# A hybrid decoder layer on one core: attention, sample and recurrent work woven between the input projections

## What is computed

```python
h = rmsnorm(x, g_mix)
z = h @ w_in                      # 1024 -> 8704 columns: xr, gr, q, k, v, g_lru, g_att
xc = causal_conv(xr)              # width 4
yr = rglru(xc, h0, w_rg_a, w_rg_x)          # gates, then a scan over time
b_lru = (yr * gelu(gr)) @ w_br_lru
q, k = rope(rmsnorm(q)), rope(rmsnorm(k))   # 12 heads of 128 each
att, kv_new = attend(q, k, v)     # 3 groups of 4 heads; samples read a cache of 1024 positions
b_att = att @ w_br_att
x = x + (sigmoid(g_lru) * b_lru + sigmoid(g_att) * b_att) @ w_out
x = x + moe(rmsnorm(x))           # top-4 of 32 experts, 12.6 MB of weights each
x = x + sigmoid(rmsnorm(x) @ w_ple_gate) * (p @ w_ple)
```

## Time and profile before

| | us |
|---|---|
| median of 3 runs (1495.41 to 1503.62) | 1499.1 |
| the profiled execution's own time | 1501.54 |
| its span, first to last instruction | 1499.7 |
| TensorE busy in it | 1367.6 (91%) |
| VectorE, ScalarE busy | 390.7, 200.4 |
| bytes moved by DMA | 530.44 MB |

### The profile page before, as it was taken

How to read it: one execution, slowest core, us unless ns; L and a number is a source line. 1 busy time by engine, 2 the same in 40 slices (tenths; PEclk the granted TensorE clock), 3 DMA queues, 4 the chain that set the end, 5 groups by cost and what they waited for, 6 DMA issues and landing times.

```text
span 1499.7 us, 16237 instructions
## 1 busy us (share of the span) xinstructions
PE 1367.6 (91%) x6662; PEld 703.2 (47%) x6662; DVE 390.7 (26%) x529; ACT 200.4 (13%) x344; POOL 18.5 (1%) x31
## 2 busy tenths in 40 slices
PE   6999996977998899999999999999999999999848
PEld 5887885866776333333333333333333333333227
DVE  2014944074223212122112212112112122121123
ACT  1113110252301110110110110110101101100001
POOL 0000000020000000000000000000000000000000
PEclk9999998998999999999999999999999999999969
DMA  9688899466445999999999999999999999999910
GB/s 374 275 333 271 297 335 365 174 214 199 193 186 210 385 412 427 428 429 428 427 429 428 428 428 428 429 428 428 428 429 429 427 428 428 429 428 428 426 49 29
DMA packets 40077, 530.44 MB, mean 354 GB/s; under 512 B 5997, under 2 KB 6141, under 8 KB 10693
## 3 DMA queue, kind: packets, MB, share of 16 engines
q1 hardware_dynamic: 36992, 470.67, 75.6%
q10 hardware_dynamic: 1685, 54.43, 9.4%
q0 software_dynamic: 1360, 4.76, 1.4%
HBM read 525.08 MB, written 58.38 MB: 389 GB/s over the span
## 4 chain that ended last, share of the span: by engine, by line
DMA 47%; PE 46%; DVE 3%; issue 2%; ACT 1%; another core or an unknown queue 0%; ACTq 0%; SPq 0%; DVEq 0%
DMA ring<-in_wexp 43%; PE PS L734 16%; PE PS L495 13%; DMA ring<-in_win 4%; PE PS L656 3%; PE PS L873 2%; PE PS L674 2%; PE PS L780 1%; PE PS L506 1%; PE PS L538 1%; PE PS L749 1%; PE PS L602 1%; DVE ring L1171 1%; PE PS L706 1%; PE PS L522 0%
## 5 line engine op out<-in xcount | busy, mean ns | idle before, releaser
L734 PE MATMUL PS<-ring,Zb 128*64 128x512 f32 x3072 | 687.3, 597 | 42.5 <-DMA ring<-in_wexp 39.3
L734 PEld LDWEIGHTS PS<-ring,Zb 128*64 128x64 f32 x3072 | 210.7, 137 | 469.9 <-issue 371.2
L495 PE MATMUL PS<-hT,ring 128*128 128x264 f32 x1024 | 233.8, 392 | 11.6 <-DMA ring<-in_win 11.6
L495 PEld LDWEIGHTS PS<-hT,ring 128*128 128x128 f32 x1024 | 197.9, 194 | 47.1 <-issue 12.5
L1374 DVE COPY Zb<-PS 64x512 f32<-64x512 f32 x32 | 21.9, 683 | 317.7 <-PE PS L734 317.7
L1037 ACT ACTIVATE Zb<-Zb 128x512 f32<-128x512 f32 x32 | 20.1, 629 | 449.5 <-DVE Zb L1352 449.5
L780 PE MATMUL PS<-Zb 128*128 128x264 f32 x256 | 75.7, 419 | 3.9 <-DVE xc L1342 2.4
L1342 DVE TENSOR_TENSOR xc<-xc,PS 128x528 f32<-128x528 f32 x68 | 47.7, 701 | 109.0 <-PE PS L780 102.1
L780 PEld LDWEIGHTS PS<-Zb 128*128 128x128 f32 x256 | 44.1, 192 | 59.4 <-issue 48.7
L1029 ACT ACTIVATE Zb<-PS 128x512 f32<-128x512 f32 x32 | 19.1, 597 | 362.8 <-PE PS L763 362.8
L1363 DVE TENSOR_SCALAR Zb<-PS 128x512 f32<-128x512 f32 x32 | 22.1, 691 | 155.2 <-PE PS L734 155.2
(11 more groups left out here) (228 smaller groups left out, 825.7 us busy)
## 6 DMA issues: line engine op xcount, KB each, us to landing
ring<-in_wexp SPq DMA_DIRECT2D x192, 2048.0 KB, 24.4
ring<-in_win SPq DMA_DIRECT2D x17, 2048.0 KB, 15.6
out_kvs<-in_cache ACTq DMA_DIRECT2D x8, 4032.0 KB, 25.1
out_kvs<-in_cache ACTq DMA_DIRECT2D x8, 1984.0 KB, 12.7
ring<-in_kt SPq DMA_DIRECT2D x2, 2048.0 KB, 14.7
ring<-in_cache SPq DMA_DIRECT2D x2, 2048.0 KB, 8.6
ring<-in_w_br_lru SPq DMA_DIRECT2D x2, 2048.0 KB, 14.9
ring<-in_w_out SPq DMA_DIRECT2D x2, 2048.0 KB, 14.9
```

Source lines behind the costliest of these rows:

```text
L495: last = mm(PS[:, t, 0:T], w[:, k, t * P:(t + 1) * P], hT[:, k, :], start=(k == 0), stop=(k == KT - 1))
L734: last = mm(PS[CAP * h:CAP * (h + 1), bank, :], src[:, k, f:f + CAP], w[:, k, h * CH:(h + 1) * CH], start=(not seeded and slot % 2 == 0 an ...
```

## The change

The parts of the program that stood one after the other are threaded through the projection. What it does, in the order of the program:

- The columns of z come as q, k, x, v, gate, merge gates. Three ring slots carry `w_in`; the fourth (`stream`, slot 3) carries one after another the cached keys of the three groups, the gate weights, the cached values of the three groups, and half of w_br_lru.
- q and k are normalized and rotated apart (`normed(0)`, `normed(1)`), each with its own sums on TensorE after tiles 13 and 25. The convolution comes behind both on VectorE.
- The samples are spread over four column groups, 8 rows of each in use; their scores stand after tiles 25, 28 and 31, their values in attention rounds 1 to 3.
- The key rows stand after tile 39, gates and value rows after tile 43. ScalarE, no longer VectorE, copies the rows out.
- Each attention round holds three of the last 24 projection tiles: scores, two tiles, transposes, one tile, product with v. The recurrent stage is spread over VectorE's and ScalarE's rounds.
- b_lru now comes before b_att, and the merged sum is made tile by tile, so that w_out starts on the first.
- Two cache copies of 4 MB and the three remainder copies move from ScalarE's queue ahead of the experts to SyncE's queue behind the first tile of the last projection; four of the other 4 MB copies move to later points.
- `further` nests its four tests, so that the first that fails skips all.
- At the end the last experts' sums use four PSUM banks in place of two (`SPREAD_AT`), ScalarE scales x tile by tile for the last projection, VectorE adds the eight squares so that one matmul sums them, and seven banks (`PG_AT`) take the projection.

The diff, cut to its core:

```diff
-ZQ, ZK, ZX, ZGR, ZV, ZGL, ZGA, NZ = 0, 12, 24, 32, 40, 52, 60, 68
+ZQ, ZK, ZX, ZV, ZGR, ZGL, ZGA, NZ = 0, 12, 24, 32, 44, 52, 60, 68
+RING = (5, 3, 2, 0, 1, 4)
+SPREAD_AT = (2, 0, 2, 0)
+PG_AT = (5, 6, 7, 0, 1, 2, 3, 5)
...
-            for c in range(1, NCHUNK):
+            def passes(c):
                 with eng.If(eng.value_load(most, min_val=0, max_val=T) > c * CAP):
...
+                    if c + 1 < NCHUNK:
+                        passes(c + 1)
+            passes(1)
...
# SyncE
+            def piece(p):
+                if p >= 3:
+                    sp.wait_ge(S.z_done, 4 * (p - 2))
+                win(p, p % 3).then_inc(wins[p % 3], 16)
+            sp.dma_start(kts[0], a["kt0"]).then_inc(S.kt0_in, 16)
+            for p in range(3, 9):
+                piece(p)
+            sp.wait_ge(S.ss_mm, 1)
+            sp.dma_start(kts[1], a["kt1"]).then_inc(S.kt1_in, 16)
+            piece(9)
+            sp.wait_ge(S.ss_mm, 2)
+            sp.dma_start(kts[2], a["kt2"]).then_inc(S.kt2_in, 16)
+            piece(10)
+            sp.wait_ge(S.ss_mm, 3)
+            sp.dma_start(stream, a["wrg"]).then_inc(S.wrg_in, 16)
+            for p in range(11, 14):
+                piece(p)
+            sp.wait_ge(S.gate_mm, 16)
+            sp.dma_start(vts, cached_v(0)).then_inc(S.v0_in, 16)
+            piece(14)
+            sp.wait_ge(S.spv_mm, 1)
+            sp.dma_start(vts, cached_v(1)).then_inc(S.v1_in, 16)
+            piece(15)
+            sp.wait_ge(S.spv_mm, 2)
...
+            sp.wait_ge(S.pg_mm, 1)
+            for g in range(NG):
+                shift_rest(sp, g)
+            for b in range(EARLY, NS):
+                shift(sp, 2, b)
...
# TensorE
+            z_tiles(4, 14)
+            qk_sums(0)
+            z_tiles(14, 26)
+            qk_sums(1)
+            stream_scores(0)
+            z_tiles(26, 29)
+            stream_scores(1)
+            z_tiles(29, 32)
+            stream_scores(2)
+            z_tiles(32, 36)
+            pe.wait_ge(S.ss_prod, 1)
...
+            z_tiles(36, 40)
+            token_rows(0)
+            z_tiles(40, 44)
+            gates()
+            token_rows(1)
+            for it in range(8):
+                n = STEP + 3 * it
+                scores(it)
+                z_tile(n)
+                z_tile(n + 1)
+                turn(it)
+                z_tile(n + 2)
+                weigh(it)
+                if 1 <= it <= 3:
+                    stream_values(it - 1)
...
-            pe.wait_ge(S.merged, 1)
+                            pe.wait_ge(S.merged, k + 1)
...
# ScalarE, ahead of the experts and at the end
-            for b in range(EARLY, NS):
-                shift(2, b)
-            for g in range(NG):
-                shift_rest(g)
...
+            for k in range(KT):
+                act.wait_ge(S.added, 2 * E + 1 + k // 2)
+                A(hT[:, k, :], xc[:, k, :], ACT.Copy, scale=feat[:, k, FGP:FGP + 1]).then_inc(S.hp_ok, 1)
```

More of the change, by code:

```diff
@@ L400, in _ @@
-            half(a["w_br_lru"], 0, wbl[0], S.wbl_in)
-            half(a["w_br_lru"], 4, wbl[1], S.wbl_in)
-            half(a["w_out"], 0, wout[0], S.wout_in)
-            sp.wait_ge(S.ba_mm, KT)
+            piece(0)
+            sp.dma_start(cst[:, :], a["cst"]).then_inc(S.cst_in, 16)
+            piece(1)
+            piece(2)
+            sp.dma_start(gqk[:, :], a["gqk"]).then_inc(S.rope_in, 16)
+            sp.wait_ge(S.xgain, 1)
+            sp.wait_ge(S.sq_ok, 1)
+            sp.dma_start(rope, a["rope"]).then_inc(S.rope_in, 16)
@@ new lines, in _ @@
+            piece(16)
+            sp.wait_ge(S.spv_mm, 3)
+            half(a["w_br_lru"], 0, wbl[0], S.wbl_in)
+            sp.wait_ge(S.z_done, 4 * 15)
+            half(a["w_br_lru"], 4, wbl[1], S.wbl_in)
+            sp.wait_ge(S.z_done, 4 * 16)
+            half(a["w_br_att"], 0, wba, S.wba_in)
+            sp.wait_ge(S.z_done, NZ)
+            half(a["w_out"], 0, wout[0], S.wout_in)
+            sp.wait_ge(S.at_pv, 8)
+            sp.wait_ge(S.tk_out, 16 * KV_STORES)
+            sp.wait_ge(S.vt_out, 16 * KV_STORES)
@@ L555, in _, with qk_sums @@
-            for g in range(NG):
-                last = mm(PS[0:32, 5, g:g + 1], prod[:, g * 32:(g + 1) * 32], ones[:, 0:1], start=True, stop=True)
-            last.then_inc(S.ss_rows, 1)
-            n = 0
-            for z0 in (ZK, ZV):
+            def qk_sums(m):
+                pe.wait_ge(S.sq_qk, m + 1)
+                for c in range(7):
+                    i = 7 * m + c
+                    n = min(CH, 12 * T - c * CH)
+                    if i >= 3:
+                        pe.wait_ge(S.qkn_ev, i - 2)
+                    mm(PS[:, 4 + i % 3, 0:n], ones, sq_qk[m][:, c * CH:c * CH + n], start=True, stop=True).then_inc(S.qkn_mm, 1)
@@ L570, in _, with gates @@
                         n += 1
+            def gates():
+                pe.wait_ge(S.wrg_in, 16)
+                pe.wait_ge(S.conv_done, 1)
+                pe.wait_ge(S.tk_ev, 9)
+                for j in range(KT):
+                    for m in range(2):
+                        n = 2 * j + m
+                        if n >= 3:
+                            pe.wait_ge(S.gate_ev, n - 2)
+                        for c in range(2):
+                            last = mm(PS[:, 4 + n % 3, 0:T], wrg[:, m, j // 2, c, (j % 2) * P:(j % 2 + 1) * P],
+                                      xc[:, 2 * (j // 2) + c, :], start=(c == 0), stop=(c == 1))
+                        last.then_inc(S.gate_mm, 1)
             def scores(it):
@@ L584, in scores, with turn @@
                 last.then_inc(S.at_sc, 1)
[L586 to L588 removed]
+            def turn(it):
                 pe.wait_ge(S.at_p, it + 1)
@@ L641, in _ @@
-            pe.wait_ge(S.spv_ev, 1)
-            pe.wait_ge(S.at_s, 8)
-            for g in range(NG):
-                last = mm(PS[:, 0, 0:32], pvrows[:, :], ident[0:96, 32 * g:32 * g + 32],
-                          start=(g == 0), stop=(g == NG - 1))
-            last.then_inc(S.spv_sum, 1)
-            def dense(weights, arrived, src, nk, done, evac, base=1):
+                if 1 <= it <= 3:
+                    stream_values(it - 1)
+                if it == 5:
+                    pe.wait_ge(S.spv_ev, 1)
+                    nc.tensor.transpose(PS[:, 7, 0:P], pvrows[:, :], ident).then_inc(S.spv_sum, 1)
@@ L650, in dense @@
+            def dense(weights, src, nk, done, evac, bank):
                 for m in range(KT):
@@ new lines, in _ @@
+            evacs(14, 16)
+            both(3)
+            evacs(16, 20)
+            both(4)
+            evacs(20, 24)
+            both(5)
+            evacs(24, 26)
+            qk_roots(1)
+            evacs(26, 28)
+            both(6)
+            evacs(28, 32)
+            both(7)
+            evacs(32, 36)
+            shift(act, 2, 0)
+            evacs(36, 40)
+            rows_out(0)
+            shift(act, 2, 1)
+            evacs(40, 44)
+            act.wait_ge(S.sp_exp, 1)
+            act.wait_ge(S.ss_rows, 1)
```

706 lines of the change are left out of this document (352 added, 354 removed).

## The result

The changed kernel takes 1480.3 us (median of 4 runs, 1477.3 to 1481.3) against 1498.5 for the kernel before, run on the same chip. The ratio is 0.987, with a 95% interval of 0.985 to 0.990: faster by 1.3%. The forecast was 1452, so the sign and the range were right and less than half of the gain came: 18 us in place of 47.

A forecast was written before the change was run, and what follows sets the result against it. The experts were taken as a DMA-bound block of fixed length, with TensorE's chain ahead of it setting its start. Gains of 25.6 (front), 2 (experts) and 19.5 (tail) summed to 47.1 us, giving 1452 us, range 1430 to 1483.

The forecast's parts named there:

- the term on the second group's values: Attention rounds: cached values land in 19.3 us behind one 4 MB copy; TensorE waits 6.6, plus 2.6 of slow clock.
- a first expert product after 485: Sign set beforehand: the weave forecast is wrong if the first expert product comes after 485 us or before 455.
- the loads set the pace: Rival, chance 0.14: both rotation transfers at 21.4 us give 1475, or the second group's values at 38.1 give 1471.
- The transfers for the rotation: Ahead of the experts: each transfer for rotating q and k taken at 10 us, between bounds of 5 and 21.4.
- TensorE's waits: At the rotations: 5.4 us ahead of the sums of k, plus 2.6 slow clock; 0.8 ahead of the samples' own scores.
- The second group's keys: One slot for seven loads: wait for the second group's cached keys between 0 and 4 us, taken as 2.
- The work: TensorE's queue from 32.76 us to the branch projections: 305.8 us of work, ending at 338.6 without waits.
- that rival: Rival, chance 0.04: column groups don't overlap, so the samples' weight loads take 39 us in place of 12, giving 1479.
- the 25.6 forecast: Front: experts start 25.6 us earlier, with the branch projections starting 21.2 earlier.
- The experts: Two 4 MB copies and the remainders leave the stretch ahead of the experts: 2 us gained, bounds 0 and 4.
- The tail: After the experts: 19.5 us gained, 13.9 from fewer branches, 2.5 from four banks, 3.1 from one matmul for squares.
- They fit by 1.7, no more: Tail: the moved copies finish at 1478.5 on the old clock, against an end of 1480.2.

The follow-up runs named there:

- run 11: Changed kernel with the recurrent state's stores and residual load deferred, and the three cache copies cut into halves of 2 KB pieces: 1453.4 us, ratio 0.969.
- run 2: Changed kernel with the recurrent state's two stores and the residual's load waiting until the branch projections have begun, cache copies unmoved: 1467.5 us, ratio 0.980.
- run 1: Changed kernel with three 4 MB cache copies issued after attention rounds 5, 6 and 7 instead of 1, 2 and 4: 1449.2 us, ratio 0.970.
- run 3: Changed kernel with cache copies after rounds 5 to 7 and the state's stores and residual load after the branch projections' start: 1443.4 us, ratio 0.964.
- run 5: Changed kernel with the four nested tests put one after the other again on every engine: 1498.6 us, ratio 0.999 to the kernel before.
- run 4: Changed kernel with the tail's two 4 MB copies and remainders issued by ScalarE behind the attention rounds: 1473.2 us, ratio 0.985.
- run 6: Changed kernel with the tail's copies issued without their wait for the last projection's first tile: 1479.6 us, ratio 0.987.
- run 7: Changed kernel with cache copies after rounds 3, 5, 7, state's stores and residual deferred, keys squared earlier, tail's copies without their wait: 1427.3 us, ratio 0.953.
- run 9: Changed kernel with only the recurrent state's 4 KB store in 4-byte pieces waiting until the branch projections have begun: 1465.8 us, ratio 0.980.

## Why the prediction was right and wrong

**The step that failed** is the term on the second group's values: "If the copy goes first, 19.3: a wait of 6.6 and 2.6 of slow clock." The mechanism was right, a load with small packets gets little until large ones are through, and run 11 shows it. The size was wrong: landing 47.1, wait 34.7. The term counted the one copy issued ahead of the load and took 10.7 us for it. The next one followed at 277.56, just when TensorE came to the values, and had to be let through too: 32.0 with both copies and nothing else (run 2). There the first copy landed at 283.0 and the second, issued at 281.54, at 300.9. Between the two, from 282 to 285, the load's queue moved 525 packets, 1.08 MB; beside the second, from 290 to 295, it moved 31 packets, 0.09 MB, against 31 packets and 2.00 MB of the copy. And the term left out GpSimd's queue: the state's store falls into the same microseconds, since the weave has moved the scan there, and made 15 more. The trace of before had a sign of it. Its stretch from 340 us on, where the store and its two companions ran alone:

```profile
340.00:353.00 13.00, 10.61 (x79) 9.20 (x81) 5.50 (x14) 3.36 (x8) 2.34 (x3) 0.66 0.66 86
```

They moved 86 GB/s at a share of 0.66, with nothing beside them to be held up; the prediction didn't use this row. By its own sign, a first expert product after 485, it was wrong on the weave: 486.77.

The rival "the loads set the pace" had the right mechanism with 38.1 for that load, 1471. It was nearer, and was given 0.14. The nearest row for a load behind copies was that 38.1; the sum took a value built from bandwidth instead.

**The other waits.** The transfers for the rotation were taken at 10; VectorE waited 13.86 and 11.43 for them. TensorE's waits came to 9.7 and 4.1 (forecast 5.4, with 2.6 of slow clock, and 0.8): a mis-sized term, 5 us even with the measured slow clock left out. The second group's keys: 1.5 for 2.0. The third group's values: none, for 0.6.

**The work.** TensorE was busy 300.3 us from 31.6 to 384.5, slow clock included, where the sum had 305.8. Column groups do overlap: 64 records with the values took 1.91 us, so that rival fell. From the branch projections to the first expert 8.3 us went (110.5 to 102.3), for 4.4 forecast. So the front's miss adds up: waits 28.8 longer than forecast, less 5.5 of work, 1.2 of an earlier start and 3.9 behind the branch projections, is 18.2, the 25.6 forecast less the 7.4 that came.

**The experts.** First product to last weights is 926.1, against 923.9 before and forecast 2 shorter; in runs 1 and 3 it is 924.4 and 926.2. The copies' leaving gave nothing that shows. First product to last projection was 948.5, close to the 947 of the text.

**The tail.** Three branches fewer: 13.9 forecast, and 14.8 idle and 16.4 in all by run 5. "They fit by 1.7, no more" was wrong: it set the copies against the end, but the result's stores are issued from 1453.2 to 1468.3, behind copies of which the last landed at 1475.5. The stores waited for them; run 4 prices this at 7.1. So the tail's two errors cancelled in part, 15.9 for 19.5.

**Luck.** That the sign and the range held is no merit of the weave: its front gave 7.4 of 25.6, and run 5 shows that without the nested tests nothing would have been gained.

Run 11's 1453 and run 1's 1449 lie near the forecast of 1452 and do not prove its sum: they have no wait or 7 us where it had 9, and 5 us more in the rotation.

What stays open is why a store of 4-byte pieces holds the other queues so long (1 GB/s from 275 to 280).

## What to carry to other kernels

A load that the critical engine waits for is priced by what else is queued in its microseconds, on every queue, GpSimd's small stores and the copies issued while it is under way included; take the row of a load that met the same company, not bytes over bandwidth. When a chain of work is moved, list where each of its stores and background copies lands in the new order, and issue bulk copies where no one waits (run 1 won 31 us by issuing three copies later). A test whose blocks are skipped costs TensorE a taken branch each; nest them, and keep bulk copies away from that moment.

## What the runs showed of the hardware

- A taken branch on TensorE took 3.4 to 4.3 us where no bulk copies ran, and 9.75 and 9.33 us beside 4 MB copies (runs 6 and 7). The Trainium skill (Runtime: NRT & Kernel Launch, Instruction fetch mechanics) says that a taken branch out of the window must first fetch its page by DMA; the traces agree in that the price moves with the DMA traffic; that the target lay out of the window here no run shows. ScalarE's and VectorE's branches stayed under 0.1 us.
- Packets of 52 KB on one queue slowed a 2 MB load of 2 KB packets from 7.5 us to 32.0; in 2 KB packets the same copies slowed it to 19.8. The two queues moved packets one for one, 25 to 23 and 351 to 349 in the same 5 us (runs 2 and 11).
- A 4 KB store in 4-byte pieces added 12.5 us to a load that also met such copies (34.6 to 47.1, run 9). Without copies, it and the two transfers behind it slowed the next 2 MB load from 8.1 us to 19.1 (runs 3 and 1); a load that had landed 4 us after the store's issue lost nothing.
